# The triangular inverse of a delta rule on Trainium2: moving operands of 32 columns a chunk instead of 64, and stationary ones spread by a mask on VectorE

## The reference

```python
A = jnp.where(strict, jnp.einsum("bnhid,bnhjd->bnhij", kb, kc) * gamma, 0.0)
eye = jnp.eye(C, dtype=jnp.float32)          # C = 64, N = 8 chunks, H = 8 heads
T = lax.linalg.triangular_solve(A + eye, jnp.broadcast_to(eye, A.shape),
                                left_side=True, lower=True)
u = jnp.einsum("bnhij,bnhje->bnhie", T, vc * bc[..., None])
w = jnp.einsum("bnhij,bnhjd->bnhid", T, kb * eG)
```

## Time and profile before

| | us |
|---|---|
| median of 3 runs | 2522.05 |
| lowest and highest run | 2521.44, 2522.14 |
| the profiled execution's own time | 2520.09 |
| its span in the trace | 2518.3 |

### The profile page before, as it was taken

The page is one execution under the profiler, slowest core; times in us unless marked ns, Lnnn a source line. Parts: engine busy times, 40 slices in busy tenths (PEclk is TensorE's granted clock), DMA queues, the critical chain, the costliest instruction groups (busy, mean ns, idle before and its releaser), DMA issues.

```text
span 2518.3 us, 37877 instructions
## 1 busy us (share of the span) xinstructions
PE 2481.8 (99%) x15440; PEld 2070.1 (82%) x15440; DVE 1619.7 (64%) x2585; ACT 1205.7 (48%) x2030; POOL 75.2 (3%) x114
## 2 busy tenths in 40 slices
PE   9999999999999999999999999999999999999998
PEld 7999888888877777878999888777776788888887
DVE  6888348866764554357887257766877655677733
ACT  6556244666555455245555246544333454444421
POOL 0111000000000000000110000000000000000000
PEclk9999999999999999999999999999999999999999
DMA  5776332222222222333775323211111112333232
GB/s 173 175 179 154 108 100 92 77 76 75 84 68 68 76 66 77 91 92 101 176 177 151 98 93 101 76 41 37 44 43 52 59 55 88 94 99 101 88 100 72
DMA packets 80525, 237.82 MB, mean 94 GB/s; under 512 B 8928, under 2 KB 10976, under 8 KB 80352
## 3 DMA queue, kind: packets, MB, share of 16 engines
q1 hardware_dynamic: 68832, 213.56, 27.0%
q0 software_dynamic: 10080, 18.35, 4.8%
q10 hardware_dynamic: 1440, 3.49, 0.4%
HBM read 233.27 MB, written 2.10 MB: 93 GB/s over the span
## 4 chain that ended last, share of the span: by engine, by line
PE 92%; DVE 5%; DMA 2%; ACT 1%; issue 1%; SPq 0%; ACTq 0%; DVEq 0%
PE bank L2208 22%; PE bank L2210 21%; PE bank L2209 21%; PE bank L2222 4%; PE bank L2224 4%; PE bank L2223 4%; PE bank L2441 2%; PE bank L2366 1%; PE bank L2280 1%; PE bank L2374 1%; DMA raw<-in_w2u 1%; PE bank L2360 1%; PE bank L2537 1%; PE bank L2347 1%; PE bank L2258 1%
## 5 line engine op out<-in xcount | busy, mean ns | idle before, releaser
L2208 PE MATMUL bank<-uR,hl 128*128 128x512 f32 x1684 | 685.4, 407 | 5.3 <-DVE uR L2954 2.8
L2943 DVE TENSOR_TENSOR hl<-raw,hl 128x1024 fp32r<-128x1024 f32 (+2 forms) x325 | 386.0, 1191 | 453.9 <-ACT hl L2586 452.8
L2210 PE MATMUL bank<-uR,hl 128*128 128x512 f32 x1684 | 658.3, 391 | 0.0
L2209 PE MATMUL bank<-uR,hl 128*128 128x512 f32 x1684 | 657.7, 391 | 0.0
L2586 ACT CAST hl<-raw 128x1024 fp32r<-128x1024 f32 (+2 forms) x325 | 329.8, 1020 | 207.2 <-PE bank L2210 196.1
L2208 PEld LDWEIGHTS bank<-uR,hl 128*128 128x128 f32 x1684 | 316.8, 188 | 94.8 <-issue 24.8
L2209 PEld LDWEIGHTS bank<-uR,hl 128*128 128x128 f32 x1684 | 317.1, 188 | 67.6 <-issue 7.2
L2210 PEld LDWEIGHTS bank<-uR,hl 128*128 128x128 f32 x1684 | 316.5, 188 | 67.7
L2937 DVE TENSOR_TENSOR hl<-raw,hl 128x1024 fp32r<-128x1024 f32 (+1 forms) x142 | 150.8, 1076 | 32.4 <-ACT hl L2582 29.4
L2222 PE MATMUL bank<-sum,hl 128*128 128x256 f32 x560 | 159.3, 284 | 2.5 <-DVE fA L3082 2.5
L2223 PE MATMUL bank<-sum,hl 128*128 128x256 f32 x560 | 158.7, 283 | 0.0
(11 more groups left out here) (499 smaller groups left out, 4385.5 us busy)
## 6 DMA issues: line engine op xcount, KB each, us to landing
raw<-in_win SPq DMA_DIRECT2D x147, 512.0 KB, 3.5
raw<-in_w SPq DMA_DIRECT2D x44, 512.0 KB, 3.5
raw<-in_w1u SPq DMA_DIRECT2D x54, 256.0 KB, 3.0
raw<-in_w2u SPq DMA_DIRECT2D x51, 256.0 KB, 3.1
raw<-in_w1g SPq DMA_DIRECT2D x22, 512.0 KB, 4.5
raw<-in_w2g SPq DMA_DIRECT2D x22, 512.0 KB, 4.3
raw<-in_w1d SPq DMA_DIRECT2D x16, 512.0 KB, 3.6
raw<-in_wssd SPq DMA_DIRECT2D x16, 512.0 KB, 3.5
```

What stands on the lines that cost most here:

```text
L2208: e.matmul(s.bank[:, :], h[:, 0, w], hi, start=s.first and q == 0, stop=False)
L2209: e.matmul(s.bank[:, :], h[:, 0, w], lo, start=False, stop=False)
L2210: i = e.matmul(s.bank[:, :], h[:, 1, w], hi, start=False, stop=s.last and q == n - 1)
L2943: e.tensor_tensor(h[:, 1, w], x[:, w], h[:, 0, w].bitcast(F), ALU.subtract).then_inc(*sig("dve_split.lo", s, i))
```

## The change

The inverse's matrices have half of their columns at zero or foreseeable at each place, and the change keeps the moving operands in 32 columns a chunk. Tm and U each get a narrow form of 256 columns (Tm itself, and Uc), in which the left and the right half of a chunk's columns lie on each other; both share one page, TU. The stationary operands stay 64x64. ScalarE copies the narrow product Yc, 256 columns, out of the bank. VectorE spreads it to the wide Y by a multiplication with a mask (`half32`, for the last level `first32`), and it spreads Uc to the wide U in the same way after each of the first four folds. The transposing matmuls of the seed take a 32-column identity. At the last level U's right half alone is subtracted from. `gdn_fold` now waits for Yc and the wide U before its product for Tm, and for the wide Y and Uc before its product for U. The constants get 36 columns, a small buffer `gy` of two pages is new, and the planner's costs for these steps are set anew.

```diff
@@ -70,8 +70,9 @@
 NPAR = _layout()
 
 CCOLS = {"ident": (0, 128), "ssdmask": (128, 128), "dist": (256, 512), "reset128": (768, 512),
-         "neg": (128, 128), "incl64": (256, 64), "id64": (320, 64), "level": (384, 384), "reset64": (768, 512), "stack": (1280, 32), "guard": (1312, 128)}
-NCA, NCB = 1440, 1280
+         "neg": (128, 128), "incl64": (256, 64), "id64": (320, 64), "level": (384, 384), "reset64": (768, 512), "eye32": (1280, 32), "half32": (1312, 2), "first32": (1314, 2),
+         "stack": (1280, 32), "guard": (1312, 128)}
+NCA, NCB = 1440, 1316
...
 O1024, O512, O128, O1 = range(4)
@@ -174,7 +175,7 @@
     if k == "sp_soft":
         return [("DVE", 0.25 + 0.09 * (s["f"]["i"] + 1), "dve_spa.P")]
     if k == "gdn_fold" and s["lev"] == 5:
-        return [("PE", 1.07), ("DVE", 0.69, "dve_gdn.U")]
+        return [("PE", 0.6), ("DVE", 0.42, "dve_gdn.U")]
...
@@ -226,10 +227,10 @@
...
-    "gdn_seed": [("DVE", 1.4, "dve_gdn.U0"), ("DVE", 0.66, "dve_gdn.A", 0), ("DVE", 0.66, "dve_gdn.A", 1)],
-    "gdn_seed_turn": [("PE", 1.15), ("ACT", 0.6, "act_gdn.T")],
-    "gdn_level": [("PE", 1.07, "pe_gdn.Y"), ("ACT", 0.6, "act_gdn.Y"), ("DVE", 0.5, "dve_gdn.mask")],
-    "gdn_fold": [("PE", 2.14, "pe_gdn.fold"), ("DVE", 0.69, "dve_gdn.T"), ("DVE", 0.69, "dve_gdn.U")],
+    "gdn_seed": [("DVE", 1.4, "dve_gdn.U0"), ("DVE", 0.36, "dve_gdn.Uc"), ("DVE", 0.66, "dve_gdn.A", 0), ("DVE", 0.66, "dve_gdn.A", 1)],
+    "gdn_seed_turn": [("PE", 0.7), ("ACT", 0.4, "act_gdn.T")],
+    "gdn_level": [("PE", 0.6, "pe_gdn.Y"), ("ACT", 0.4, "act_gdn.Yc"), ("DVE", 0.62, "dve_gdn.Y"), ("DVE", 0.6, "dve_gdn.mask")],
+    "gdn_fold": [("PE", 1.15, "pe_gdn.fold"), ("DVE", 0.42, "dve_gdn.T"), ("DVE", 0.42, "dve_gdn.U"), ("DVE", 0.62, "dve_gdn.wide")],
...
     with ExitStack() as ph:
         con[1] = sb(ph, "con2", [128, NCB])
         fB[1] = sb(ph, "fB2", [128, NB2, L])
+        gy = sb(ph, "gy", [128, 2, 256])
         with ExitStack() as gxs:
             gx = sb(gxs, "gx", [128, 16, L])
         mR[1] = sb(ph, "mR2", [128, 16, L], R)
@@ -343,6 +345,15 @@
...
+
+    def narrow8(x):
+        return x.rearrange("p (c l) -> p c l", c=C8)
+
+    def wide8(p):
+        return p[:, :].rearrange("p (c i l) -> p c i l", c=C8, i=2)
+
+    def over32(name):
+        return cc(1, name)[:, None, :, None].broadcast_to([128, C8, 2, 32])
...
@@ -1695,7 +1706,8 @@
     fp.left += [(b, t_phase) for b in wide_pages(fB[1], NB2)]
     kp = Pages([gx[:, 2 * i:2 * i + 2, :].rearrange("p i l -> p (i l)") for i in range(3)], "pairs of gx pages")
     gp = Pages([gx[:, i, :] for i in range(6, 16)], "gx pages")
-    for pool in (kp, gp):
+    yp = Pages([gy[:, i, :] for i in range(2)], "gy pages")
+    for pool in (kp, gp, yp):
         pool.left = [(b, t_phase) for b, _ in pool.left]
...
         yield from ready(AT)
-        U, Tm, Y, Ak, Ak2 = gp.take(), gp.take(), gp.take(), gp.take(), gp.take()
-        s4 = step("gdn_seed", AT=AT, U=U, A=[Ak, Ak2])
+        yield from until(lambda: yp.left)
+        U, TU, Y, Ak, Ak2, Yc = gp.take(), gp.take(), gp.take(), gp.take(), gp.take(), yp.take()
+        Tm, Uc = TU[:, 0:256], TU[:, 256:512]
+        s4 = step("gdn_seed", AT=AT, U=U, Uc=Uc, free=list(TU.after), A=[Ak, Ak2])
         yield from ready(("dve_gdn.U0", s4), banks=1)
         b = SB.take()
-        s5 = step("gdn_seed_turn", U=U, Tm=Tm, b=b, s=s4)
+        s5 = step("gdn_seed_turn", U=U, Tm=Tm, free=list(TU.after), b=b, s=s4)
         b.release(("act_gdn.T", s5))
-        Tm.t, U.t = [("act_gdn.T", s5)], [("dve_gdn.U0", s4)]
+        tT, tU, tW = ("act_gdn.T", s5), ("dve_gdn.Uc", s4), ("dve_gdn.U0", s4)
         At = [("dve_gdn.A", s4, 0), ("dve_gdn.A", s4, 1)]
         yield
         wY = list(Y.after)
         for lev in range(1, 6):
             A = (Ak, Ak2)[(lev + 1) % 2]
-            yield from ready(At[(lev + 1) % 2], Tm, banks=1)
-            b = SB.take()
-            s6 = step("gdn_level", lev=lev, A=A, at=At[(lev + 1) % 2], AT=AT, Tm=Tm, tt=list(Tm.t), Y=Y, free=wY, b=b)
-            b.release(("act_gdn.Y", s6))
+            yield from ready(At[(lev + 1) % 2], tT, banks=1)
+            b, small = SB.take(), lev < 5
+            s6 = step("gdn_level", lev=lev, A=A, at=At[(lev + 1) % 2], AT=AT, Tm=Tm, tt=tT, Y=Y, Yc=Yc, free=wY, b=b)
+            b.release(("act_gdn.Yc", s6))
             if lev < 4:
                 At[(lev + 1) % 2] = s_mask = ("dve_gdn.mask", s6)
-            yield from ready(("act_gdn.Y", s6), U, banks=2)
+            if small:
+                yield from ready(("act_gdn.Yc", s6), tW, banks=2)
+            yield from ready(("dve_gdn.Y", s6), tU, banks=2)
             b = SB.take()
-            b2 = SB.take() if lev < 5 else None
-            s7 = step("gdn_fold", lev=lev, Y=Y, U=U, ut=list(U.t), Tm=Tm, tt=list(Tm.t), s=s6, b=b, b2=b2)
+            b2 = SB.take() if small else None
+            s7 = step("gdn_fold", lev=lev, Y=Y, Yc=Yc, U=U, Uc=Uc, ut=tU, wt=tW, Tm=Tm, tt=tT, s=s6, b=b, b2=b2)
+            tU = ("dve_gdn.U", s7)
             if lev < 5:
-                Tm.t = [("dve_gdn.T", s7)]
-                b2.release(*Tm.t)
-            U.t = [("dve_gdn.U", s7)]
-            b.release(*U.t)
+                tT, tW = ("dve_gdn.T", s7), ("dve_gdn.wide", s7)
+                b2.release(tT)
+            b.release(tU)
             wY = [("pe_gdn.fold", s7)]
             yield
-        Tm.release(("pe_gdn.Y", s6))
+        U.t = [tU]
+        TU.release(*wY)
+        Yc.release(*wY)
         Y.release(*wY)
         Ak.release(("pe_gdn.Y", s6))
...
         def gdn_turn_v(s):
             turn_pair(s, "pe_gdn.v")
 
-        def blocks64(b, x, y):
+        def blocks32(b, x, y):
             for c in range(C8):
-                at = slice(c * 64, c * 64 + 64)
                 for r in HALF:
-                    i = e.matmul(b[r, at], x[r, at], y[r, at], start=True, stop=True)
+                    i = e.matmul(b[r, c * 32:c * 32 + 32], x[r, c * 64:c * 64 + 64], y[r, c * 32:c * 32 + 32], start=True, stop=True)
             return i
 
         def gdn_seed_turn(s):
             go.wait_ge(*on("dve_gdn.U0", s.s))
             after(*s.b.after)
+            eye = cc(1, "eye32")
             for c in range(C8):
-                at = slice(c * 64, c * 64 + 64)
                 for r in HALF:
-                    i = e.matmul(s.b[r, at], s.U[r, at], con[1][r, r], start=True, stop=True)
+                    i = e.matmul(s.b[r, c * 32:c * 32 + 32], s.U[r, c * 64:c * 64 + 64], eye[r, :], start=True, stop=True)
             i.then_inc(*sig("pe_gdn.seed", s))
 
         def gdn_level(s):
-            after(s.at, *s.tt, *s.b.after)
-            blocks64(s.b, s.A, s.Tm).then_inc(*sig("pe_gdn.Y", s))
+            after(s.at, s.tt, *s.b.after)
+            blocks32(s.b, s.A, s.Tm).then_inc(*sig("pe_gdn.Y", s))
 
         def gdn_fold(s):
-            go.wait_ge(*on("act_gdn.Y", s.s))
-            after(*s.ut)
             if s.lev < 5:
-                after(*s.b2.after)
-                blocks64(s.b2, s.U, s.Y).then_inc(*sig("pe_gdn.foldT", s))
-            after(*s.b.after)
-            blocks64(s.b, s.Y, s.U).then_inc(*sig("pe_gdn.fold", s))
+                go.wait_ge(*on("act_gdn.Yc", s.s))
+                after(s.wt, *s.b2.after)
+                blocks32(s.b2, s.U, s.Yc).then_inc(*sig("pe_gdn.foldT", s))
+            go.wait_ge(*on("dve_gdn.Y", s.s))
+            after(s.ut, *s.b.after)
+            blocks32(s.b, s.Y, s.Uc).then_inc(*sig("pe_gdn.fold", s))
 
...
 
         def gdn_seed_turn(s):
             go.wait_ge(*on("pe_gdn.seed", s))
-            after(*s.Tm.after)
-            e.copy(s.Tm[:, :], s.b[:, :]).then_inc(*sig("act_gdn.T", s))
+            after(*s.free)
+            e.copy(s.Tm, s.b[:, 0:256]).then_inc(*sig("act_gdn.T", s))
 
         def gdn_level(s):
             go.wait_ge(*on("pe_gdn.Y", s))
-            after(*s.free)
-            e.copy(s.Y[:, :], s.b[:, :]).then_inc(*sig("act_gdn.Y", s))
+            after(*(s.free if s.lev > 1 else s.Yc.after))
+            e.copy(s.Yc[:, :], s.b[:, 0:256]).then_inc(*sig("act_gdn.Yc", s))
...
             e.tensor_tensor(v8(s.U), chunks8(cc(1, "id64")), v8(s.U), ALU.subtract).then_inc(*sig("dve_gdn.U0", s))
+            go.wait_ge(*on("dve_gdn.U0", s))
+            after(*s.free)
+            e.tensor_tensor(narrow8(s.Uc), wide8(s.U)[:, :, 0, :], wide8(s.U)[:, :, 1, :], ALU.add).then_inc(*sig("dve_gdn.Uc", s))
             for n in range(2):
...
 
         def gdn_level(s):
+            go.wait_ge(*on("act_gdn.Yc", s))
+            after(*s.free)
+            e.tensor_tensor(wide8(s.Y), narrow8(s.Yc[:, :])[:, :, None, :].broadcast_to([128, C8, 2, 32]),
+                            over32("half32" if s.lev < 5 else "first32"), ALU.mult).then_inc(*sig("dve_gdn.Y", s))
             if s.lev < 4:
                 at = CCOLS["level"][0] + 64 * (s.lev + 2)
-                go.wait_ge(*on("pe_gdn.Y", s))
```

(19 more changed lines are left out.)

## The result

The changed kernel takes 2553.31 us (median of 4 runs, 2551.57 to 2561.05), the kernel before 2521.74 beside it (2521.16 to 2522.14). The ratio is 1.0131, interval [1.0110, 1.0153]: slower by 33 us by the ratio, where I had said 2521 and a range up to 2532.

The account below looks back on a forecast made before the run. TensorE, busy 99% of the span, was taken as the bound; -2.6 (TensorE), -1.7 (ScalarE) and +3.6 (VectorE) gave -0.7 us from 2522.05, so 2521 us, range 2510 to 2532.

Parts of the forecast that it names:

- The TensorE part: Inverse's matmul blocks: weight loads set the spacing, so halved streams save little; -2.6 us, between 0 and -4.1.
- the halved block: Rival for the inverse's blocks: streams set the pace and a block halves; 2493 to 2513, likeliest 2506 us, chance 0.09.
- halving the stream alone buys nothing: Step for the inverse's blocks: with 64 stationary columns the spacing stays about 56 ns a pair.
- TensorE's work: -2.6: Sum for the inverse's blocks: -1.4 us from spacing and -1.2 from the ends of runs of blocks.
- That only changes the order: Planner's table, 0.6 us for a block expected at 1.0: claimed to change only the order, no cost counted.
- the rival at 2514: Rival: the new order removes stalls in the side-only stretches; about 2514 us, 2508 if all go, chance 0.14.
- The VectorE part: Added VectorE work, 15.8 us in all, hidden by gemm except in three side-only stretches; +3.6 us, range 0 to +9.7.
- will put off more of it: Top-k in the last side-only stretch: planner moves more to 1897 to 1940 us, so half is charged, +1.6 us.
- The ScalarE part: Copies of Y and the transpose shrink from 584 to 368 ns; eight TensorE waits shorten by 0.216 us, -1.7 us.
- VectorE as the bound: Rival: VectorE bounds the side-only stretches, 2529 us; 2531 with one more low-clock stretch of 1.7 us; chance 0.27.
- C: Cause tested in the follow-ups, not forecast: 32-column streams bring TensorE's low clock; expected 26 of the 35 us.
- O: Cause tested in the follow-ups, not forecast: the new instruction order, planned from other costs, leaves gaps that lower the clock.

Follow-up runs that it names:

- the old order: The whole change with planner costs set so that TensorE's list is the kernel before's but for 19 lines, 32-column streams: 2544.94 us, ratio 1.0099.
- the five instructions alone: Kernel before with only five added VectorE instructions at a level in each pair, 14 us of work, nothing else changed: 2529.50 us, ratio 1.0042.
- wide streams in the old order: The whole change with TensorE's list as in the kernel before but for 19 lines, each narrow chunk given twice (64 columns): 2528.22 us, ratio 1.0033.
- one program: Kernel before with 32-column streams, half of the inverse's products left out: two runs at 2531, three at 2547 us, ratio of all 1.0089.

## Why the prediction was wrong

**The TensorE part: its price was right, and it left out the clock.** The load does set the spacing: 60 against 58 ns a pair, 1.08 against 1.05 us a block (1627.65 to 1628.70), loads unchanged at 135 ns, nowhere the 0.55 us of the halved block. That is the section "LDWEIGHTS (loading the stationary operand)" of "TensorE: Matmul & The Clock Gate" in the Trainium skill, and the runs agree with it. The step that failed is the sentence "halving the stream alone buys nothing": the spacing stays and the clock doesn't. I had the low clock only as a short consequence of a gap (2.00 us idle at 1869.91), and priced it in one rival at 1.7 us. The runs show that with 32 columns the low level behind a gap lasts: some 37 us in place of 7 after the same 2.00 us, 26 us in place of under 5 after 3.2, though TensorE is busy nearly all of them. And they show it fall, near 1727 in the changed kernel and 1719 in the old order, behind gaps of 0.56 us and less. "TensorE's work: -2.6" had no term for this; the thin streams measured +11.8 in the new order and +16.6 in the old one. What makes the clock fall in the one case and not in the other stays open.

**"That only changes the order", costed at nothing.** This step failed too. The order alone costs 14.4 us with TensorE's new costs in the kernel before, 8.1 to 12.9 in the changed one, 13 with the masks on GpSimd, and 5.0 after a cost moved by 0.07. I had counted new orders only as a gain (the rival at 2514). Of the six other orders in these runs none was faster than the old one with the same instructions. Why the old one is the best of them isn't shown.

**The VectorE part: mechanism right, size too small.** The work came to +16.8 us for +15.8, and it showed where VectorE was full. I took +3.6 of a range 0 to 9.7; the five instructions alone cost 10.6, the change's own set 8.3 with ScalarE's share in it. With the -1.7 of the ScalarE part taken as I had it, VectorE's part would be about 10, at the top of my bound. That the planner "will put off more of it", to 1897 to 1940 "where VectorE has room", came true in its first half: the top-k was put off, to 2001 to 2019, and the weight split stood behind it, 8.65 us. What was late next I hadn't asked. But planning it earlier lost 18 us more, so the 8.65 can't simply be taken off the rest.

**The ScalarE part.** The copies went from 584 to 371 ns, as read from the nearest row. Its -1.7 was never measured by itself.

The rival that came nearest was VectorE as the bound (2529 to 2531): with wide streams in the old order that case is 2528.2, against 2519.4 for the kernel before on that chip. The remaining 24.7 us are C and O. Both of the prediction's own signs came, "if a side-only stretch grows by over 4 us, or if new gaps near 1900 to 1980 appear because masks of the top-k come late". The first stretch without gemm lasts 31 us (1711.8 to 1743.1), where it had 21. And one of the new gaps ends at 1973.79: the scan's state update (L3475) stood in VectorE's queue behind the top-k's last rounds and its mask, which is made from L3561 on. TensorE's row, then two of VectorE's:

```profile
1973.79 0.45 PE L2508 MATMUL bank<-fB,fA 128*64 128x128 f32 x1 [3.67 <-DVE fB L3475]
```

```profile
1969.54 0.61 DVE L3561 TENSOR_SCALAR_CACHE_REDUCE fA<-fB,small 128x384 f32<-128x384 f32 x1
...
1973.04 0.60 DVE L3475 SCALAR_TENSOR_TENSOR fB<-fB,small,bank 128x128 f32<-128x128 f32 x2
```

What stays open: why one program shows two levels (2531 and 2547), and why relief of VectorE brought nothing while load cost at once.

## What to carry to other kernels

In this kernel matmuls that are spaced by their loads gained nothing from fewer moving columns and lost TensorE's clock. So before thinning streams, look for stretches that have nothing else for TensorE, and price them also at the duration that the same block has in a row at the low clock (1.92 here for 1.12 us). In a kernel whose order comes from a planner, a changed cost is a change by itself: run the new order with the old instructions and the new instructions in the old order before judging either. Work added to an engine that is 90% busy in a stretch should be given a price (here 8.3 to 14.1 us of time for 14 to 25 us of work), and the room that some other work leaves by moving has a price where that work lands.

## What the hardware showed that I hadn't expected

TensorE's granted clock was 0.55 in the mean of a window in which it was busy 28.8 of 29 us, most of it with blocks of 32 moving columns. In the old order it was 0.50 with 32 columns and 10.00 of 10 us busy, and 1.00 with 64 columns and 7.07 of 10. Behind the same 2.00 us gap the low level lasted 7 us with 64 columns and 37 with 32. GpSimd's product of 128x512 took 1307 ns in the mean, in the kernel with the old order, against 686 on VectorE in the kernel before, and nothing waited for it:

```profile
L3630 POOL TENSOR_TENSOR gx<-gx,con 128x512 f32<-128x512 f32 x12 | 15.7, 1307 | 522.3 <-PE bank L2441 522.3
```
